# Sample units woven between prompt heads, and a bias read in natural order

## The reference

```python
logits = einsum(q, k) * HEAD_DIM ** -0.5
bias = rel_bias[bucket(qpos - kpos)]          # one table per head
p = softmax(where(mask, logits + bias, -1e30))
o = gates[0] * o_c + gates[1] * o_s + gates[2] * o_w
h = h + rmsnorm(o @ w_o)
```

## Time and profile before

| | us |
|---|---|
| median of 3 runs | 2641.81 (2641.01 to 2641.97) |
| profiled execution | 2639.05 |
| its span | 2637.50 |
| TensorE busy | 2548.4 (97%) |
| VectorE busy | 1221.3 (46%) |
| ScalarE busy | 909.8 (34%) |
| POOL busy | 282.4 (11%) |
| mean granted TensorE clock | 0.984 of full |

### The profile page before, as it was taken

The page is one execution under the profiler, slowest core; times in us unless marked ns, Lnnn a source line. Parts: engine busy times, 40 slices in busy tenths (PEclk is TensorE's granted clock), DMA queues, the critical chain, the costliest instruction groups (busy, mean ns, idle before and its releaser), DMA issues.

```text
span 2637.5 us, 44257 instructions
## 1 busy us (share of the span) xinstructions
PE 2548.4 (97%) x17430; PEld 2486.8 (94%) x17430; DVE 1221.3 (46%) x1384; ACT 909.8 (34%) x1124; POOL 282.4 (11%) x316
## 2 busy tenths in 40 slices
PE   8799999999999999999999989899999999999997
PEld 6789999999999999899997779899999999999997
DVE  6654444444444444644435644644444444444444
ACT  3344323323332333532323633533233223323332
POOL 2420000000000001300001311300000000000012
PEclk9899999999999999999999999999999999999998
DMA  6524444444444444444453364334444444344443
GB/s 249 181 91 144 155 163 143 146 155 160 145 159 157 149 153 147 143 144 143 146 213 118 103 202 143 116 140 144 158 159 154 151 157 157 134 164 164 143 151 127
DMA packets 82202, 400.25 MB, mean 152 GB/s; under 512 B 8188, under 2 KB 18812, under 8 KB 52194
## 3 DMA queue, kind: packets, MB, share of 16 engines
q1 hardware_dynamic: 81570, 390.06, 42.9%
q0 software_dynamic: 576, 9.47, 1.0%
HBM read 391.80 MB, written 15.82 MB: 155 GB/s over the span
## 4 chain that ended last, share of the span: by engine, by line
PE 86%; DVE 6%; ACT 3%; issue 2%; SPq 1%; DMA 1%; POOL 1%; DVEq 0%; ACTq 0%
PE ps L1259 27%; PE ps L1261 27%; PE ps L1260 27%; ACT w_hi L464 1%; DVE w_lo L710 1%; PE ps L1345 1%; SPq L349 1%; PE ps L1431 1%; DVE winB L817 1%; DVE winA L817 0%; DMA pastK<-win_k_dram 0%; PE ps L1279 0%; PE ps L1281 0%; PE ps L1503 0%; ACT sq L498 0%
## 5 line engine op out<-in xcount | busy, mean ns | idle before, releaser
L1259 PE MATMUL ps<-x_hi,w_hi 128*128 128x320 f32 x3536 | 1097.6, 310 | 13.8 <-DVE w_lo L710 9.9
L1260 PE MATMUL ps<-x_lo,w_hi 128*128 128x320 f32 x3536 | 1095.3, 310 | 0.0
L1261 PE MATMUL ps<-x_hi,w_lo 128*128 128x320 f32 x3536 | 1095.0, 310 | 0.0
L710 DVE TENSOR_TENSOR w_lo<-w_raw,w_hi 128x2048 fp32r<-128x2048 f32 (+1 forms) x365 | 751.3, 2058 | 662.6 <-ACT w_hi L464 662.6
L464 ACT CAST w_hi<-w_raw 128x2048 fp32r<-128x2048 f32 (+1 forms) x365 | 624.5, 1711 | 539.1 <-PE ps L1261 474.0
L1259 PEld LDWEIGHTS ps<-x_hi,w_hi 128*128 128x128 f32 x3536 | 666.5, 188 | 16.2 <-DVE w_lo L710 9.7
L1260 PEld LDWEIGHTS ps<-x_lo,w_hi 128*128 128x128 f32 x3536 | 666.5, 188 | 0.4 <-issue 0.2
L1261 PEld LDWEIGHTS ps<-x_hi,w_lo 128*128 128x128 f32 x3536 | 666.3, 188 | 0.0
L1259 PE MATMUL ps<-hid_hi,w_hi 128*128 128x320 f32 x1408 | 435.2, 309 | 0.3 <-DVE w_lo L710 0.3
L1260 PE MATMUL ps<-hid_lo,w_hi 128*128 128x320 f32 x1408 | 435.1, 309 | 0.0
L1261 PE MATMUL ps<-hid_hi,w_lo 128*128 128x320 f32 x1408 | 435.1, 309 | 0.0
(11 more groups left out here) (238 smaller groups left out, 1527.7 us busy)
## 6 DMA issues: line engine op xcount, KB each, us to landing
w_raw<-w_in_dram SPq DMA_DIRECT2D x176, 1024.0 KB, 4.9
w_raw<-w_out_dram SPq DMA_DIRECT2D x128, 704.0 KB, 4.0
w_raw<-w_kv_dram SPq DMA_DIRECT2D x24, 1024.0 KB, 4.9
w_raw<-w_q_dram SPq DMA_DIRECT2D x17, 1024.0 KB, 4.8
w_raw<-w_o_dram SPq DMA_DIRECT2D x16, 1024.0 KB, 4.8
win_out_dram<-win_kv_dram POOLq DMA_DIRECT2D x8, 992.0 KB, 5.3
rowsK<-cmp_data_dram SPq DMA_DIRECT2D x16, 256.0 KB, 9.2
w_raw<-w_pool_dram SPq DMA_DIRECT2D x4, 1024.0 KB, 6.4
```

The costliest lines, as they stand in the source:

```text
L710: V.tensor_tensor(w_lo[:, slot, 0:width], w_raw[:, slot, 0:width], w_hi[:, slot, 0:width].bitcast(F32), ALU.subtract).then_inc(lo_made, 1)
L1259: M(out, wh, xh[:, k, :], start=(k == 0), stop=False)
L1260: M(out, wh, xl[:, k, :], start=False, stop=False)
L1261: last = M(out, wl, xh[:, k, :], start=False, stop=(k == kt - 1))
```

## The change

The order of units becomes head, sample, head; head, sample, head; and so on. `p` is a place in that order, `unit(p)` the unit. All semaphores of the steps count places. One buffer remains each for past keys and values. The bias comes to DRAM as each head's row repeated 128 times (row length `NL` = 392), in eight DMAs on POOL's queue, one after each of the query tiles 0 to 7; reads with a step of `NL - 1` then give the natural order, `biasP` in two halves and `bias_s` directly, and the reversing products are gone. The three branches of a sample keep their places, but compressed keys of all four key heads (60 columns) are scored together with the foreign ones masked by `biasSC` (60 columns, -1e30 outside a head's own 15), and the compressed values are one 60-row block. ScalarE takes `vP`, `vN`, and `vCP` copies. The second output panel is loaded to the region Y, over queries that are no longer needed, during the steps, and both panels' high halves are in the last steps.

```diff
-    bias_dram = nc.dram_tensor("bias_by_distance", (NH, NE), F32, kind="Internal").ap()
+    bias_dram = nc.dram_tensor("bias_by_distance", (NH, P, NL), F32, kind="Internal").ap()
...
+    def unit(p):
+
+        b, k = divmod(p, 3)
+        return NH + b if k == 1 else 2 * b + k // 2
...
+        sp.wait_ge(trow_out, 16 * (NH // 2))
+        sp.dma_start(bias_s[:, :], bass.AP(t, DS - 1, [[P * NL, NH], [NL - 1, DS], [1, PAST + DS]])).then_inc(bias_s_in, 16)
...
+            sp.dma_start(biasP[:, bias_at(h0):bias_at(h0) + NH // 2, :],
+                         bass.AP(t, h0 * P * NL + PAST + DS - 1 - P, [[NL - 1, P], [P * NL, NH // 2], [1, SEQ]])).then_inc(bias_in, 16)
+
         sp.wait_ge(lo_made, P_WO)
         sp.dma_start(w1Kp[:, :, :], cmp_w1[0]).then_inc(w1Kp_in, 16)
+        sp.wait_ge(tile_made, P_WO - 1 + TOFF)
+        bias_half(0)
         sp.wait_ge(tile_made, P_WO + TOFF)
+        bias_half(1)
...
+            if b:
+                sp.wait_ge(s_made, place(NH + b - 1) + 1)
...
+            if b:
+                sp.wait_ge(o_made, place(NH + b - 1) + 1)
...
+        for b in range(DB):
+            load_keys(b)
+            load_values(b)
+            if b == 0:
+                sp.wait_ge(crow_sum, 2)
+                panel(P_WO, 0, w_o[0], PW)
+            if b == DB // 2:
+                sp.wait_ge(s_made, place(PW // NT) + 1)
+                sp.dma_start(w_rawY[:, :], w_o[1]).then_inc(raw_in[(P_WO + 1) % 2], 16)
```

VectorE, between the sums of the compressed rows (`crow_copy`, `cmp_join` and `link` are as before):

```diff
+        crow_copy(0, 1)
         cmp_join(2, 3, NKV, False)
...
         dve.wait_ge(mask_set, 1)
+        dve.wait_ge(bias_s_in, 16)
+        V.tensor_copy(bias_n[:, DB - 1, :], bias_s[:, PAST:PAST + DS])
...
+        dve.wait_ge(bias_in, 32)
         V.tensor_copy(biasC[:, 1, :, :], biasP[:, :, CB - 1:SEQ:CS])
...
+        crow_copy(1, 0)
+        cmp_join(3, 2, NKV, False)
         dve.wait_ge(kc_sum, 2)
+        V.tensor_copy(kcP[:, :], ps[:, 3, 0:NKV * NCMP]).then_inc(kc_made, 1)
```

POOL's writes, and TensorE's preparation and steps:

```diff
+        for n in range(NH // 2):
+            pool.wait_ge(tile_made, P_Q + TOFF + n + 1)
+            pool.dma_start(bias_dram[2 * n:2 * n + 2, :, :], rep(trow[2 * n:2 * n + 2, 0:NL], P)).then_inc(trow_out, 16)
...
+        crow_part(1, w1Vp, 0, CS).then_inc(crow_sum, 1)
+        pe.wait_ge(w1Kp_in, 16)
+        crow_part(0, w1Kp, 0, 6)
+        turn_sums(0, 1)
         pe.wait_ge(sig_made, 1)
...
+        crow_part(0, w1Kp, 6, CS).then_inc(crow_sum, 1)
+        turn_values(0)
+        turn_values(1)
+        turn_sums(1, 0)
+        pe.wait_ge(gates_made, 1)
+        turn_values(2)
+        turn_values(3)
         pe.wait_ge(cmp_hid, 4)
+        M(ps[:, 3, 0:NKV * NCMP], w2[:, 0, :], hcP[:, 0, :], start=True, stop=True).then_inc(kc_sum, 1)
         pe.wait_ge(kc_made, 2)
...
+        def values_of(p):
+
+            b = unit(p) - NH
+            if p >= 2:
+                pe.wait_ge(o_read, p - 1)
+            M(ps[0:NC4, 6 + p % 2, 2 * P:3 * P], hcS[:, 1, b * NC4:(b + 1) * NC4], w2[:, 1, :],
+              start=True, stop=True).then_inc(vc_sum, 1)
...
         for s in range(UNITS + 4):
             if s < UNITS:
                 scores(s)
+            if s == 0:
+                compressed_values()
+            if s == 1:
+                new_values()
+            if s == 2:
+                pe.wait_ge(vcp_made, 1)
+                pe.wait_ge(vt_made, 5)
+            if is_sample(s - 4):
+                turn_outputs(s - 4)
             if 2 <= s < UNITS + 2:
                 transposes(s - 2)
             if 3 <= s < UNITS + 3:
                 outputs(s - 3)
+            if is_sample(s - 2):
+                values_of(s - 2)
```

More of the change, by code:

```diff
@@ L80 @@
 NE = SEQ + PAST + DS - 1
+NL = PAST + SEQ - P + DS
 def plan_sbuf(nc):
@@ L291, in bias_at, with place, is_sample @@
         return (u + NH // 2) % NH
-    def out_bank(u):
-        return 6 + (u + 1) % 2 if u < NH else 6
+    def unit(p):
+        b, k = divmod(p, 3)
+        return NH + b if k == 1 else 2 * b + k // 2
+    def place(u):
+        return 3 * (u - NH) + 1 if u >= NH else 3 * (u // 2) + 2 * (u % 2)
+    def is_sample(p):
+        return 0 <= p < UNITS and unit(p) >= NH
     ext_s = ext[:, :, EXT_P:EXT].rearrange("p c (b j) -> p c b j", b=DB)
@@ L420, in _ @@
[L420 to L436, removed]
+                sp.dma_start(pastV[:, 0, p, :], slc_kv[page(b * NPG + p), :, 1, :]).then_inc(pastV_in, 16)
@@ L634, in _, with copy_vP, exps @@
         A(gT[:, :], gT[:, :], ACT.Sigmoid).then_inc(sig_made, 1)
+        def copy_vP(n):
+            act.wait_ge(vt_sum, n + 1)
+            nc.scalar.copy(vP[:, n // 2, n % 2, :], ps[:, 4 + n, :]).then_inc(vt_made, 1)
         gelu(2, 1, hcP[:, 1, :])
+        copy_vP(0)
+        copy_vP(1)
         gelu(3, 0, hcP[:, 0, :])
[L640 to L646, removed]
+        copy_vP(2)
+        copy_vP(3)
+        act.wait_ge(kc_sum, 3)
+        nc.scalar.copy(vCP[0:NCMP, :], ps[0:NCMP, 4, :]).then_inc(vcp_made, 1)
+        def exps(p):
+            act.wait_ge(max_made, p + 1)
+            if p >= 3:
+                act.wait_ge(rec_made, p - 2)
+            s3 = p % 3
+            for n, (lo, w) in enumerate(SPANS_S if is_sample(p) else SPANS_P):
                 last = A(sc[:, s3, lo:lo + w], sc[:, s3, lo:lo + w], ACT.Exp, bias=neg[:, s3, n:n + 1],
@@ L1211, in _ @@
         last.then_inc(qS_made, 1)
-        for u in range(UNITS):
-            s3 = u % 3
-            pool.wait_ge(rec_made, u + 1)
+        for p in range(UNITS):
+            s3 = p % 3
+            pool.wait_ge(rec_made, p + 1)
             o, f = sc[:, s3, :], rec[:, s3, :]
-            if u < NH:
+            if not is_sample(p):
                 v = pick(o, 0, 272, 2, NCMP)
@@ L1517, in scores, with transposes @@
                     M(ps[rows, a + br, PAST:PAST + NEW], q, kT(br, v)[:, SEQ:NT], start=True, stop=True)
[L1518 to L1530 removed]
+            M(ps[:, a, PAST + NEW:PAST + NEW + NC4], qS[:, b, :, :].rearrange("p h i -> p (h i)"),
+              kcS[:, b * NC4:(b + 1) * NC4], start=True, stop=True).then_inc(s_made, 1)
+        def transposes(p):
+            pe.wait_ge(p_made, p + 1)
+            if p:
+                pe.wait_ge(pTa_made, p)
+                pe.wait_ge(pTb_made, p)
+            o = sc[:, p % 3, :]
+            if not is_sample(p):
                 for n, lo in enumerate((16, 288, 144, 544)):
```

360 lines of the change are left out of this document (157 added, 203 removed).

## The result

The changed kernel takes 2676.18 us (median of 4 runs, 2675.68 to 2676.96) against 2641.41 for the kernel before beside it: a ratio of 1.0135, interval 1.012 to 1.015. Forecast was 2623, so the sign was wrong as well as the size. The profiled execution took 2676.44 us over a span of 2674.9, 37.4 more than before; TensorE is busy for 2545.5 of them, 2.9 less than before. The added time is waiting.

The account below looks back on a forecast made before the run. Outside attention, weight streaming stays as is; the 166.5 us attention stage loses time in preparation and to late keys in its tail. Gains of 12.5 in preparation and 6.2 in steps: 2641.8 - 18.7 = 2623 us, range 2611 to 2634.

Parts of the forecast that it names:

- I cost that at nothing: Query tiles: the high half starts when TensorE releases it, so row writes beside query panel loads cost 0.
- a panel's landing doubled to 9.6: Query tiles, worst case: panels land 2.6 beyond the 7.04 of a tile in eight tiles, some 20 us.
- (C): Rival: SyncE's wait for all eight row writes, ahead of `w1Kp`, makes it slower, 2635 to 2951 us; chance 0.07.
- Part 1: Preparation, up to the first scores: flip products and waits removed, first scores at 1407.8 instead of 1420.34, 12.5 us gained.
- D: Rival in preparation: bias halves land after 1403 and VectorE waits; gain 12 at 20 us; counted within the forecast's 0.72.
- Part 2: Steps, to the first output tile: 14.4 us for three steps, two prompt and one sample; 6.2 us gained.
- second cycle: Steps, set by the single buffer: key load 10.8, scores 1.3, transposes 0.9, outputs 1.4, so 14.4 for three steps.
- (B): Rival in the steps: both cycles add and key landings stretch; 16.5 a cycle, 2637, no measurable change; chance 0.09.
- The steps' total: Steps: 6.2 of the 18.7 us gained, with the first output tile at 1537.9 against 1556.56.
- late landing: Steps: keys land 5.99 us after issue instead of 5.16, making three steps 15.2 instead of 14.4.
- the wait of the values product for `x_lo`: Steps: TensorE's values product waits for `out_low` of two units before, 1.0 us, raising three steps from 13.1 to 14.1.
- `w_rawY` at 3.2: Steps: the 1-MB load issued once between values(4) and keys(5) adds 3.2 of its 4.8 us.

Follow-up runs that it names:

- dram_two_rows: Changed kernel with the rows put in DRAM once and repeated from there by eight DMAs, the two rows still outermost: 2639.43 us, ratio 0.9992.
- all_three: both_order plus the rows put in DRAM once and repeated from there with the 128 repeats outermost: 2617.48 us, ratio 0.991 to the kernel before.
- copy_first: Changed kernel with VectorE copying a sample's compressed values ahead of the step's scores: 2658.47 us, ratio 1.0065 to the kernel before.
- both_order: copy_first plus SyncE issuing the next sample's keys before the values: 2651.0 us, ratio 1.0037 to the kernel before.
- all_late: all_three with the product of the compressed values one step later on TensorE, behind the new scores: 2615.8 us, ratio 0.9901 to the kernel before.

## Why the prediction was wrong

**Where it failed first: "I cost that at nothing".** The sentence on the query panels saw the right meeting, writes beside panels, and took "a panel's landing doubled to 9.6" as the worst, some 20 us. Panels took up to 27.4. The slack was misread too, in the other direction: 9.7, not 7.04. A doubled landing would hardly have cost anything: in `dram_two_rows` panels take 8.0, the longest 9.3, and no tile is late. The bound was what was wrong. It came from the landing of a panel alone, and had no price for what a write takes of the engines, although the sum for (C) had one within reach: on two of 16 lanes a write needs 15.0 us (its 401 KB are thousands of bytes, the 392 KB of the profile). A write measured 56 us of engine time, which is 28 on two engines, and the last one landed in 23.0.

**Rival (C) had the mechanism and the wrong place.** It gave (C) to SyncE's wait for all eight writes ahead of `w1Kp`, and a lane share of 15 to 30 us. The last landing, 23.0, and the 28 by engine time fall in that range. But the writes mostly overlap, and the last, issued at 1364.8, landed at 1387.8 of a stage that ended at 1426. `w1Kp` went out at 1416.6, 9.7 before the sums as in the kernel before: the place named never decided. The price was paid by the query panels, whose bytes go through the same engines. Rival (C) at 0.07 was too low, and so was every chance for slower.
The Trainium skill ("DMA: Bandwidth & Descriptors", section "Rules for kernel authors") says that an outermost dimension of fewer than 16 confines a DMA to at most that many engines and advises a multiple of 16 outermost. The trace agrees: one write by two rows holds 13.2% of the 16 engines' time, where two engines are 12.5%.
The prediction drew from the same page of the Trainium skill (section "Why a DMA increments its semaphore by 16 and not by 1") that two engines carry a write, that the next write goes to other engines, and so that the writes overlap. The trace agrees, with 24.9% for two writes under way. The prediction went on to say that each panel's share on two engines is delayed; that half was the one that mattered, and no price was put on it.

**Part 1, preparation, was right.** Forecast 12.5, measured 12.4. In `all_three`, where nothing delays the sums, the first scores are at 1407.8, the figure forecast. The bias reads cost nothing (D not seen).

**Part 2, the steps: cycle 14.4 forecast, 16.5 measured.** The step that failed is the second cycle, "from the end of outputs(b-1) to keys landed: 10.8 ... then scores 1.3, a head's transposes 0.9, outputs of b 1.4". By the chain above: 10.5 in place of 10.8; scores 1.69 for 1.3; VectorE's work on those scores and its copy, 2.63, where transposes stood at 0.9; outputs 1.75 for 1.4. The sum moves by -0.3 + 0.4 + 1.7 + 0.35 = 2.1. The big term is an omission: outputs(b) need `copy_values`, and I hadn't asked what stands in front of that copy on VectorE. The diff shows that order. (B) had 16.5 a cycle, but by added cycles and stretched landings; the landing here was 4.98, so its number was right by luck.

**The steps' total: +15.3 for -6.2.** Of the 21.5, between the samples' scores lie 18.5: seven intervals sum to 122.5, against 7 x 14.4 + 3.2 = 104.0. Six cycles at 2.14 more make 12.8; the two intervals with the clock at 0.90 and 0.70 are 1.4 and 4.1 above 16.54; the rest is small. The end, from the last transposes to the first output tile, took 11.3 for 7.3: the outputs there are 1.60 where they are 1.08 at the full clock. What lies ahead of the first sample's scores and behind the last sample's, up to the last transposes, took 17.7 for 18.8; with that the sum closes, 18.5 + 4.0 - 1.1 = 21.4. With the copy moved (`copy_first`) the undisturbed cycles are 14.8 to 15.0, between the forecast 14.4 and its late landing, 15.2.

**Right in the steps:** the wait of the values product for `x_lo`, 1.0 each time and six times; that this wait adds to 14.1 a cycle (14.31 in `all_three`); that keys would be last by a small margin once nothing else is in the way.
**Not right there:** `w_rawY` at 3.2. With keys issued first it costs nothing, with keys last 2 to 2.5.

The intention of the change is sound by these runs: without its two faults, and with keys ahead of values, it gains 23 us over the kernel before. Keys ahead of values were no part of the change, and `both_order` priced them at 7.5; an estimate for the change without its two faults is thus 16, near the 18.7 forecast.

## What to carry to other kernels

A write off the critical path is not free because its own completion isn't waited for: work out its engine time, how many engines it goes to, and compare the delay with the slack that the loads beside it have, from issue to use. In a DMA that repeats a few rows, try a long dimension outermost (16 and 128 did it here). When units are reordered in a software pipeline, go through each engine's written order, and for each small copy ask which wait of a *newer* unit stands in front of it; such a copy made the next load wait for the one before it here.

## What the runs showed of the hardware

- Repeating rows out of SBUF cost about twice the engine time of repeating them out of DRAM: 55 to 56 us of engine time per 392 KB against 24 to 27, whatever the order of dimensions.
- One write with two rows outermost kept about two of the 16 DMA engines busy (13.2% of their time; 24.9% with two writes under way), and loads of 1 MB beside such writes out of SBUF landed in up to 27.4 us. With 16 rows outermost, same source and bytes, they landed in 4.9.
- With two rows outermost a write of 392 KB came as about 700 packets, some 600 of them under 512 bytes; with 128 or 16 outermost as about 112 (from DRAM 5664 against 928 on the queue, with the one copy of the rows). The number of packets did not set the engine time (12.9% and 14.2%).
- In intervals in which TensorE waited again and again for a microsecond or two, the granted clock was sometimes 0.70 to 0.90 of full, at 1 to 4 us each. That is a mean of 2.4 GHz and 1.2 GHz: at the end of the changed kernel's steps a pair of passes of L1591 takes 0.85, and 0.43 in `all_three` (L1599). Which interval it falls in differs from kernel to kernel. It took back what `all_late` had gained in the steps. Why it fell there and not in `all_three` stays open.
